# Delta heads: 16x16 blocks inverted on VectorE, unnormalised keys and queries, decays moved into the levels stage

## The reference, cut to what matters

```python
lower = jnp.where(strict, jnp.einsum('bhnid,bhnjd->bhnij', kb, k) * decay, 0.0)
rhs = jnp.concatenate([v * beta, kb * jnp.exp(gc)[..., None]], axis=-1)
sol = lax.linalg.triangular_solve(lower + jnp.eye(CHUNK, dtype=jnp.float32), rhs,
                                  left_side=True, lower=True, unit_diagonal=True)
...
a_intra = jnp.where(incl, jnp.einsum('bhnid,bhnjd->bhnij', q, k) * decay, 0.0)
```

## Time and profile before

| | us |
|---|---|
| median of 3 runs (2526.24 to 2527.37) | 2527.37 |
| the profiled execution | 2526.02 |
| its span, first to last instruction | 2524.5 |
| PE busy in the span | 2446.4 |
| DVE busy | 1332.0 |
| ACT busy | 992.5 |
| POOL busy | 320.8 |

### The profile page before, as it was taken

One profiled execution on the slowest core, in us unless ns is written; L12 is line 12 of the kernel. 1 busy time (PEld: TensorE's weight loads), 2 busy tenths in 40 slices (PEclk: granted clock), 3 DMA queues, 4 the chain that ended last, 5 costly groups with the idle time before them and its releaser, 6 DMA issues. The chain is left out here.

```text
span 2524.5 us, 56135 instructions
## 1 busy us (share of the span) xinstructions
PE 2446.4 (97%) x23072; PEld 2330.3 (92%) x23072; DVE 1332.0 (53%) x2347; ACT 992.5 (39%) x1908; POOL 320.8 (13%) x398
## 2 busy tenths in 40 slices
PE   7999999999999999999999999999999999999998
PEld 5889889999999999989988898899999999999898
DVE  5565653677333434663565656537773344356644
ACT  4555532333234424452365455323332353255422
POOL 1322201000012101110012222100000110011000
PEclk9999999999999999999999999999999999999999
DMA  7101114111234233124221110231113332222122
GB/s 270 46 31 40 31 37 149 43 43 51 101 106 106 81 108 99 57 63 147 76 92 46 31 40 23 69 133 34 51 50 87 88 91 83 77 68 82 55 99 84
DMA packets 55734, 193.86 MB, mean 77 GB/s; under 512 B 9080, under 2 KB 9246, under 8 KB 55376
## 3 DMA queue, kind: packets, MB, share of 16 engines
q1 hardware_dynamic: 40352, 147.34, 17.4%
q0 software_dynamic: 15152, 43.24, 6.3%
HBM read 177.97 MB, written 8.39 MB: 74 GB/s over the span
## 5 line engine op out<-in xcount | busy, mean ns | idle before, releaser
L734 PE MATMUL proj<-h_hi,w_hi 128*128 128x320 f32 x3072 | 739.5, 321 | 4.3 <-DVE h_lo L2171 2.9
L734 PE MATMUL proj<-h_lo,w_hi 128*128 128x320 f32 x3072 | 702.0, 309 | 0.0
L734 PE MATMUL proj<-h_hi,w_lo 128*128 128x320 f32 x3072 | 698.7, 309 | 1.3 <-issue 1.3
L2171 DVE TENSOR_TENSOR w_lo<-raw,w_hi 128x1024 fp32r<-128x1024 f32 x232 | 287.8, 1241 | 480.4 <-ACT w_hi L1573 479.6
L734 PEld LDWEIGHTS proj<-h_hi,w_hi 128*128 128x128 f32 x3072 | 504.1, 189 | 20.3 <-issue 5.9
L734 PEld LDWEIGHTS proj<-h_lo,w_hi 128*128 128x128 f32 x3072 | 514.8, 188 | 0.0
L734 PEld LDWEIGHTS proj<-h_hi,w_lo 128*128 128x128 f32 x3072 | 513.0, 188 | 1.6 <-issue 1.6
L734 PE MATMUL mix<-area 64*64 64x64 f32 (+6 forms) x8176 | 470.8, 236 | 11.8 <-issue 4.5
L734 PEld LDWEIGHTS mix<-area 64*64 64x64 f32 (+4 forms) x8176 | 405.0, 140 | 61.7 <-issue 36.5
L1573 ACT ACTIVATE w_hi<-raw 128x1024 fp32r<-128x1024 f32 x232 | 245.8, 1060 | 532.7 <-PE proj L734 329.7
L1573 ACT ACTIVATE area<-mix 128x256 f32<-128x256 f32 (+8 forms) x462 | 189.3, 433 | 632.9 <-PE mix L734 510.1
(11 more groups left out here) (304 smaller groups left out, 2653.7 us busy)
## 6 DMA issues: line engine op xcount, KB each, us to landing
raw<-in_w_in SPq DMA_DIRECT2D x128, 512.0 KB, 3.5
raw<-in_w_mb SPq DMA_DIRECT2D x96, 512.0 KB, 3.5
raw<-in_w_mod POOLq DMA_DIRECT2D x32, 512.0 KB, 4.7
area<-in_bias POOLq DMA_DIRECT2D x64, 128.0 KB, 4.6
raw<-in_w_out SPq DMA_DIRECT2D x16, 512.0 KB, 3.5
out_x<-area SPq DMA_DIRECT2D x10, 512.0 KB, 2.6
merged<-in_w_mod SPq DMA_DIRECT2D x8, 512.0 KB, 11.3
area<-area POOLq DMA_DIRECT2D x64, 64.0 KB, 1.9
```

Source lines behind the costliest of these rows:

```text
L734: return T.matmul(out, l, r, start=start, stop=stop)
L2171: return V.tensor_tensor(out, a_, b_, op)
```

## The change

- Keys and queries stay unnormalised. ACT writes SiLU's result straight into `kq` and its square into `A_c` (`A_squared`). PE sums the squares with 10 products with a column of ones (front u = 3). POOL takes the roots and puts them into the row factors (beta and the like); the root of the queries goes into the output's normalisation. The squares, sums and two multiplications on DVE, the transposes back and those of q are gone; the front has 10 parts.
- The doubling steps for block sizes 1, 2, 4 and 8 are gone. In their place DVE cuts the 16x16 diagonal blocks out (`A_decays`, `A_blocks`), five DMAs carry them to a layout of 40 partitions by 16x16 (`Z`; three on SP's queue, two on POOL's), DVE eliminates 14 pivots (`A_pivots`, two instructions each), five more DMAs bring the inverses back, and DVE and ACT spread them into X and Y (`A_spread`). SP's part (`relay(h)`) stands in its queue behind the load of unit 4h+7 and ahead of that of unit 4h+8.
- The decay parts of head h+1's front (u = 0 to 2) move from the scan of head h to the start of its levels. The first doubling step that is left starts after 17 eighths.
- ACT now makes `Rv` too (30 ACTIVATEs), POOL no longer. POOL masks `decT` and multiplies it with k q^T in the scan of the head before. Convolutions, `A_hi` and `A_lo` have new places.

```diff
+                def relay(h):
+
+                    sp.wait_ge(A_own.sem, A_own.at(layer, 3 * h + 2))
+                    held(sp)
+                    for t in range(SP_TILES):
+                        blocks_in(sp, t, A_relay)
+                    sp.wait_ge(A_own.sem, A_own.at(layer, 3 * h + 3))
+                    held(sp)
+                    for t in range(SP_TILES):
+                        inverses_back(sp, t, A_relay)
...
+                    root = stat[:, O_STAT:O_STAT + 5]
+                    pool.wait_ge(A_oss.sem, A_oss.at(layer, h + 1))
+                    held(pool)
+                    P.tensor_tensor(root, root, neg_half[:, 0:5], ALU.pow)
+                    held(pool)
+                    P.drain()
+                    pt(root, root, rn_q(h)).then_inc(A_orn.sem, A_orn.step)
...
+                    elif u == 3:
+                        tr(o(0), kq[:, 0, tile(4)])
+                        for i in range(2):
+                            for t in range(TILES):
+                                last = mm(o(1)[:, 5 * i + t:5 * i + t + 1], A_c[:, i, tile(t)], ones[:, 0:1])
...
+
+                    fill(0, 1)
+                    if h < HEADS - 1:
+                        A_front(h + 1, 0)
+                        A_front(h + 1, 1)
+                    fill(1, 5)
+                    if h < HEADS - 1:
+                        A_front(h + 1, 2)
+                    fill(5, 17)
+                    A_level_q(h)
+                    fill(17, 18)
+                    A_level_d(h)
+                    if h:
+                        pe.wait_ge(proj_taken.sem, proj_taken.at(layer, u0 + 2))
+                        A_out(h - 1, psum_a[(u0 + 1) % 2])
+                    fill(18, 20)
+                    A_mid_q(h)
+                    fill(20, 21)
+                    A_mid_d(h)
+                    fill(21, 22)
+                    A_last_q(h)
+                    fill(22, 23)
+                    A_last_d(h)
+                    fill(23, 24)
+                    pe.wait_ge(A_x.sem, A_x.at(layer, 5 * h + 5))
+                    pe.wait_ge(A_qn.sem, A_qn.at(layer, 6 * h + 6))
                     pe.wait_ge(A_rest.sem, A_rest.at(layer, h + 1))
...
+                    eighths(0, 3, u + 6, u + 7)
...
+                def A_squared(h):
+                    A.drain()
+                    A.activation(A_c[:, 0:2, :], kq[:, 0:2 + h % 2:1 + h % 2, :], ACT.Square).then_inc(A_qkv.sem, 2 * A_qkv.step)
...
-                    act.wait_ge(A_lat.sem, A_lat.at(layer, h + 1))
-                    act.wait_ge(A_va.sem, A_va.at(layer, 5 * h))
-                    A_level(h, 0)
                     if more:
                         A_take(h + 1, 0)
                         A_hi(4 * h + 6)
-                    for lv in range(1, 5):
-                        A_level(h, lv)
-                        A_keys(h, Rk if lv < 3 else kd, 5 if lv < 3 else 3, (lv - 1) % 2)
-                        if more and lv == 3:
-                            A_take(h + 1, 1)
-                            A_hi(4 * h + 7)
-                        if not more and lv == 2:
-                            join_gate(0)
-                            A_hi(18)
-                    A_level(h, 5)
+                        for u in range(3):
+                            A_front(h + 1, u)
+                        A_hi(4 * h + 7)
+                    else:
+                        join_gate(0)
+                        A_hi(18)
+                    act.wait_ge(A_rn.sem, A_rn.at(layer, h + 1))
+                    for d in range(2):
+                        A_keys(h, Rk, 5, d)
+                    for d in range(2):
+                        A_keys(h, Rv, 1, d, TILES)
+                    if more:
+                        A_take(h + 1, 1)
+                    act.wait_ge(A_sb.sem, A_sb.at(layer, 5 * h))
+                    for d in range(2):
+                        A_keys(h, kd, 3, d)
                     if not more:
                         join_gate(1)
...
+                    A_spread(h)
+                    A_level(h)
                     if more:
+                        A_take(h + 1, 2)
+                        A_silu(h + 1)
+                    A_mid(h)
+                    A_last(h)
+                    if more:
+                        A_squared(h + 1)
                         A_hi(4 * h + 8)
-                        A_silu(h + 1, 0, 2)
-                        A_silu(h + 1, 2, 1)
...
+
+                def A_blocks(h):
+                    dve.wait_ge(A_fev.sem, A_fev.at(layer, FRONT * h + 7))
                     dve.wait_ge(A_rn.sem, A_rn.at(layer, h + 1))
...
+                def A_pivots(first, end):
+                    for p in range(first, end):
+                        n = 15 - p
+                        below = Z[:, p + 1:16, :, 0:p]
+                        tmp = Z_tmp[:, 0:2 * n * p].rearrange("q (i d c) -> q i d c", i=n, d=2)
+                        mul(tmp, Z[:, p + 1:16, :, p:p + 1].to_broadcast([40, n, 2, p]), Z[:, p, :, 0:p].unsqueeze(1).to_broadcast([40, n, 2, p]))
+                        fence()
+                        tt(below, below, tmp, ALU.subtract)
+                        fence()
+
+                def A_inverse(h):
+                    V.tensor_scalar(ZO[:, :, 0:4:3, :], Z, -1.0, None, ALU.mult)
+                    V.tensor_scalar(ZO[:, :, 1:3, :], Z.rearrange("p i d j -> p j d i"), -1.0, None, ALU.mult).then_inc(A_own.sem, A_own.step)
...
+                def A_spread(h):
+                    dve.wait_ge(A_relay.sem, A_relay.at(layer, 6 * h + 6))
...
+                    mul(ss, ss, rn_q_sq(h))
+                    fence()
...
+                A_decays(0)
+                A_blocks(0)
+                A_lower(0)
                 A_lo(5)
-                A_lower(0)
+                A_scaled(0)
+                A_pivots(1, 4)
                 for h in range(HEADS):
                     more = h < HEADS - 1
+                    if more:
+                        A_lo(4 * h + 6)
+                    A_pivots(4, 9)
+                    A_lo(4 * h + 7 if more else 18)
+                    A_pivots(9, 15)
+                    A_inverse(h)
+                    if more:
+                        A_convolve(h + 1, 0)
                     if h:
                         A_out_squares(h - 1)
-                    dve.wait_ge(A_x0.sem, A_x0.at(layer, h + 1))
-                    update(h, 0)
+                    A_spread(h)
                     if more:
-                        A_lo(4 * h + 6)
+                        A_convolve(h + 1, 1)
+                    update(h)
                     if h:
                         A_out_normed(h - 1)
-                    update(h, 1)
+                    update_mid(h)
                     if h:
-                        A_out(h - 1, psum_a[int(h == HEADS - 1)])
-                    update(h, 2)
+                        A_out(h - 1, psum_a[(4 * h + 6 if more else 4 * HEADS + 1) % 2])
+                    update_last(h)
+                    if more:
+                        A_convolve(h + 1, 2)
                     if h:
                         split_y(h - 1, A_y, False)
...
+                    if more:
+                        A_decays(h + 1)
...
+                        if n == 1:
+                            A_blocks(h + 1)
                         elif n == 2:
-                            A_normed(h + 1)
-                        elif n == 4:
                             A_lower(h + 1)
+                        elif n == 3:
+                            A_scaled(h + 1)
+                            A_pivots(1, 4)
```

More of the change, by code:

```diff
@@ L25 @@
 LEVELS = 7
-FRONT = 14
+FRONT = 10
 SP1 = NT + 1
@@ L257, in program @@
         a_x = a.at
-        X, Y = a.take(2, TILES, 64), a.take(2, TILES, 64)
+        XY = a.take(4, TILES, 64)
+        X, Y = (XY.rearrange("p (d i) t c -> p i d t c", i=2)[:, i] for i in range(2))
         XT = a.take(2, TILES, 128)
@@ new lines, in A_front @@
+                    if FRONT * h + u >= 2:
+                        pe.wait_ge(A_fev.sem, A_fev.at(layer, FRONT * h + u - 1))
+                    if u == 3 and h:
+                        pe.wait_ge(A_wt.sem, A_wt.at(layer, h))
+                    if u in (3, 8):
+                        pe.wait_ge(A_qkv.sem, A_qkv.at(layer, 3 * h + (2 if u == 3 else 3)))
+                    par = h % 2
+                    if u < 3:
+                        for c, (d, t) in enumerate(((u, t) for t in range(4)) if u < 2 else ((0, 4), (1, 4))):
@@ L1033, in A_levels @@
                 def A_levels(h):
+                    u0 = 4 * h + 5 if h < HEADS - 1 else 4 * HEADS
                     def fill(first, end):
-                        u0 = 4 * h + 5 if h < HEADS - 1 else 4 * HEADS
-                        if h == HEADS - 1:
-                            end = min(end, 22)
-                        if first <= 8 < end and h:
-                            eighths(0, u0, first, 8)
-                            pe.wait_ge(A_ox.sem, A_ox.at(layer, h))
```

(32 more changed lines are left out.)

452 lines of the change are left out of this document (213 added, 239 removed).

## The result

The changed kernel takes 2532.06 us (median of 15 runs, 2530.07 to 2543.35), the kernel before on the same chip 2527.7 (2526.24 to 2529.43): ratio 1.0019, 95% interval 1.0012 to 1.0027. The forecast was 2513; the time lies inside the range, on the other side of no change. The profiled execution of the changed kernel is the slowest of its 15, 2543.35 us; the others reach 2535.2 at most. Its mean granted clock, the share of full speed that TensorE was given, is 0.970, that of the others 0.973 to 0.976, so its clock losses are some 10 us larger than the usual ones. In what follows a fall is a stretch in which this clock is at its lower level.

What follows compares the result with a forecast made beforehand. PE was taken as the bound, busy 2446.4 of 2524.5 us. Terms -96 + 72 + 2 + 8 = -14 against 2526.0 gave 2512, with the median 1.3 above: 2513 us; eight-in-ten range 2475 to 2548.

Steps and rivals of the forecast that it cites:

- PE's work, -96: PE, both layers: dropped steps -93, fewer filler changes -8, fewer transposes -13, added one-column products +18; -96 us.
- The waits, +72 + 2: New PE waits in mixer A, 53 us per layer against 17, +72; bare factors at each layer's end, +2.
- take: PE's wait before units 7, 11 and 15, released by ACT's take; 3.8 us in each head after a scan.
- opening: Each layer's start: front part 3 waits for ACT's squares 7.6 us, PE covers 2.3; a wait of 5.3 us.
- output norm: Heads 1 to 3: normalised output queues on DVE behind the second direction's merges; PE waits 2.1 us each.
- last head: Join gate and table load stand ahead of the high part, so the spread is late; PE waits 6.0 us.
- before the next unit: DVE's third convolution delays unit 4h+8's low part; PE waits 1.8, 2.6 and 3.2 us in heads 0 to 2.
- The spread behind the take: DVE does the output's squares before spreading; PE waits 1.6 us, then 0.9 more for ACT's half.
- The clock, +8: Slow clock behind five waits per layer of 3.8 us or more; two bare at 1.7 us each, +8 us.
- The clock falls more often: Rival: all twelve waits per layer over 1.7 us cost 1.7, 41 us instead of 8; 2546 us; chance 0.15.
- The late relay: Rival: relay DMAs land late; at 4.6 us the gain of 14 is gone, at 6.5 2543 us; chance 0.15.
- DVE's pivots: Elimination on DVE: 3.3 us for pivots 4 to 8, 3.6 for 9 to 14; dearer strided forms +18, 2531 us.

Runs made afterwards that it cites:

- keep_busy_all: Changed kernel plus TensorE products that nobody reads, ahead of both its long and its shorter waits in the head mixer; 2504.31 us.
- keep_busy: Changed kernel plus TensorE products that nobody reads, ahead of its long waits in the head mixer only; 2527.94 us.
- conv_first: Changed kernel with the next head's first convolution on VectorE ahead of pivots 9 to 14 instead of behind them; 2552.68 us.
- pivots_first: Changed kernel with all pivots and the inverse in one piece on VectorE, ahead of the low part of unit 4h+7; 2535.28 us.
- reordered: Changed kernel with the orders of VectorE, ScalarE, TensorE and the opening put together anew, nothing left out; 2494.89 us.
- before_delayed: Kernel before with six idle multiplications on VectorE ahead of the first update of heads 1 to 3 in each layer; 2554.51 us.
- before_ones: Kernel before with ten one-column TensorE products per head added, results unread, in the scan of the head ahead; 2552.09 us.

## Why the prediction was wrong, point by point

- **PE's work, -96.** Right. Take keep_busy_all, whose clock is nearly full: 2435.9 busy, less its 566 unread products at 0.147 (83 us), is 2353; the forecast was 2446.4 - 96 = 2350. Twenty one-column records took 2.3 us, two in 0.22 as taken.
- **The waits, +72 + 2.** Right in sum. Idle time in keep_busy_all with the filled part added is 70 + 83 = 153 us against 2524.5 - 2446.4 = 78 before: +75. By name in layer 0 of the changed kernel: take 3.88 (3.8 forecast), opening 5.18 (5.3), output norm 1.93 (2.1), last head 6.97 (6.0), before the next unit 1.64, 2.71, 2.78 (1.8, 2.6, 3.2). Head 0's take was 5.35 instead of 3.8; in layer 1 the three takes are 4.12 to 4.25 and the opening only 3.50. The spread behind the take cost 0.4 + 0.4 and not 1.6 + 0.9, since the slow clock had used that time up: in keep_busy, at the full clock, it costs 1.18 + 1.01. The head period in keep_busy_all is 67.3 and 68.1 us (66 to 68 forecast).
- **Two costs inside were mis-sized and hidden.** The scaling products take 2293 ns and not some 350, because POOL multiplies at the same time; DVE then had less to wait for ACT's high part (1.03 us in head 1, where 3.4 was reckoned). And an on-chip DMA of the relay lands in 2.2 us on the way in and 2.7 on the way back, where 1.9 was taken, with 0.65 us of issue each on either queue where at most 1.1 us in all was taken:

```profile
L287 SPq DMA_DIRECT2D area<-area x24: 602/647/675, 114.7 to 1587.4; - x24
DMA to landing us min/median/max: 2.6/2.7/3.2
```

  Both came out in conv_first, pivots_first and reordered, where their cover was gone.
- **The clock, +8: the step that failed.** It measured 28 us (36 in the profiled execution, 2541.8 - 2506.1). The prediction counted falls behind five waits per layer of 3.8 us and more, took three of the five as swallowed by the next wait and priced the other two at 1.7 each. The traces show falls behind about half of the waits of 1.0 to 2.8 us as well (before_delayed shows them alone, at 2.7 us), falls of 8 us behind most of the long waits where one of 1.7 us lost at half speed lasts 3.4, and falls behind one-column products with no wait at all. How the 28 divide among these was not measured. With 8 replaced by 28 the sum is 2533; the median is 2532.
- **The rivals.** "The clock falls more often" came nearest: it had twelve falls per layer, priced 41 us in all, and gave 2546, 14 too many; 28 us over its 24 waits is 1.2 each. Its mechanism holds in part, since not each of the shorter waits brings a fall and the long waits' falls last longer. The late relay did not decide in this order: the waits for the spread are 0.4 + 0.4. DVE's pivots cost what was taken (3.3 and 3.6 us for 4 to 8 and 9 to 14).

What stays open: which idle time each fall belongs to. Filling the long waits gave 4 us, the short ones none, both 28, but the two part fillings also changed the waits behind them, so they don't tell whether a fall is the affair of one wait; and the same 2.7 us wait brings one or not. Whether the one-column products, taken away without anything in their place, would give part of the 28 was not tried.

## What to carry to other kernels

Taking work off PE in a kernel that PE bounds paid here only with DVE and ACT put in a new order at the same time: the same change is worth 0.2% to the wrong side in the old order and 2.2% to the right one in the new (how much a new order alone would give the kernel before was not tried). Price a new wait on PE, of the lengths seen here, at itself plus 1.2 to 1.8 us of clock, an estimate from the mean of 24 waits here (1.2) and from six waits of 2.7 us (1.8), and test it by filling all the waits with unread products: filling a part of them moves the others. Before a wait is removed, walk on to the one that comes next (conv_first), and look what POOL reads while DVE has two operands in SBUF.

## What was not expected of the hardware

- The granted clock can fall behind 20 records of one-column products while the timeline shows PE busy for 4.00 of 4.00 us (0.67 over 218 to 222 us in before_ones; in four of its eight heads it doesn't fall). The Trainium skill ("TensorE: Matmul & The Clock Gate", Part 1) ties the clock to how busy the array has been; the rows agree only if what the timeline shows as busy is not always busy in this sense.
- Some 83 us of added matmuls (566 at 0.147) made the kernel 28 us faster.
- A 256-element product on DVE lasted up to 3.4 us beside a POOL product of 2.9 us.
